# Laying x out by chunk, reordering the first loads and norms, and splitting the convolution's norm in a conditioned decoder block

## Chip, cores and metric

The kernel runs on all 8 cores of one Trainium2 chip. Each core computes one of the 8 sequences; the cores exchange nothing. The time is the device time of one launch in microseconds, that of the slowest core.

## The reference

For one sequence, x is 2048 x 1024 and c has 1024 entries. Weights are float32; the kernel multiplies in bf16.

```
mod = silu(c) @ w_ada + b_ada              # sh1 sc1 gt1 sh2 sc2 gt2, 1024 each
h   = rmsnorm(x) * (1 + sc1) + sh1         # norm1_g folded in
p   = h @ w_in                             # u_a u_b | g_b g_c v | gates A, B
u   = (u_a + b) * sigmoid(u_b + b)
y_a = silu(layernorm(causal_conv31(u))) @ conf_w_out + b
y_b = (g_b * causal_conv3(g_c * v)) @ sc_w_out
x   = x + gt1 * ((sigmoid(gA) * y_a + sigmoid(gB) * y_b) @ w_o)
h2  = rmsnorm(x) * (1 + sc2) + sh2
x   = x + gt2 * ((silu(h2 @ w_g) * (h2 @ w_u)) @ w_down)
out = rmsnorm(x)
```

## The kernel before

Everything is kept transposed: channels on the 128 partitions, positions along the free dimension. The 2048 positions are four chunks r = 0..3 of TU = 512, the 1024 channels eight tiles k = 0..7 (KD). One matmul multiplies a 128x128 weight tile with a 128x512 tile; eight of them, over k, make one PSUM bank. Six banks go round as a ring (`next_bank`); banks 6 and 7 belong to reductions and to junk outputs.

The order of work is written out by hand in `stages()`. `Sched` notes for every operation which buffers it reads and writes, and places semaphore waits on the engine that issues it; each engine then runs its own list strictly in order. DMAs are issued from SP (the hardware queue) and from POOL (the software queue, all weight loads, which read float32 and write bf16), so a wait in either list holds back the loads behind it. A buffer that overlaps another in the one arena waits for that one's readers.

The stages, with the names used below:

- **Startup.** `load_x(r, q)` brings half a chunk of x. `crit_load(k)` brings the 1 MB of w_ada for the shift and the scale of channel tile k; `crit_group(k)` multiplies it with silu(c) in two long VectorE products and makes `gm` and `mod` of tile k in two short ones. `in_sq(r)` squares a chunk, `in_red(r, b)` sums the squares with eight matmuls by ones and makes 1/rms (Ln, Exp) on ScalarE, `in_tmp` multiplies x by it, `in_h` applies scale and shift. While these h tiles appear, matmuls are streamed, four for each (k, r) of r = 0, 1 (line 585), with slot A as weights. Slot B (`load_half(1, q)`) is issued from POOL in iteration k = 5, and `u_unit(2, 0)` is the first group that needs it.
- **Units.** `u_unit(j, r)`: 16 matmuls and the sigmoid gate (`glu`). `sc_unit(j, r)`: 24 matmuls (g_c, v, g_b), the 3-tap convolution on VectorE (one TS, two STT) and two TTs. Chunks 2 and 3 are normed by `in_sq`, `in_red`, `in_apply` between units.
- **31-tap convolution.** `load_xsh(r)` copies u into shifted rows by 16 DMAs from SBUF to SBUF. `conv_a(r)`: four groups of 32 narrow matmuls (line 627), each evicted twice by ScalarE. `conv_b(r)`: the layer norm, 8 matmuls by ones, then a chain of VectorE and ScalarE to four Silu outputs, all emitted in one piece.
- **Gates.** 32 steps (m, r) of 24 matmuls. From the units `sc_unit(3, r)` on, `bg_step()` adds three small w_ada products to each step, with three ring buffers whose loads SP issues.
- **Reload.** x is read a second time into `xs` for the residual, eight 1 MB DMAs, one per channel tile, issued after `conv_b(3)`.
- **w_o.** `wo_units(r)`: eight groups; m < 4 uses slot A, the others slot B. Then the dense FFN and the final norm.

Of the kernel before, what the change touches and what calls it, by code (L numbers as in the profile page):

```python
# [164 lines left out]
def build_nc():  # L165
    nc = bass.Bass("TRN2", target_bir_lowering=False)
    din = lambda n, s: nc.dram_tensor(n, s, F32, kind="ExternalInput").ap()
    xT = din("xT", [1024, S])
# [9 lines left out]
    with ExitStack() as st:  # L178
# [30 lines left out]
        B_xs = [[sch.buf("xs%d_%d" % (k, r), O_XS + (k * S + r * TU) * 4, O_XS + (k * S + (r + 1) * TU) * 4)  # L209
# [44 lines left out]
        B_wada = [mbuf("wada%d" % i, O_WADA + i * 8192, 8192) for i in range(NWR)]  # L254
        wada_sem = [dsem("d_wada%d" % i) for i in range(NWR)]
        cact = f32ap(O_CBF, 1024); B_cact = xbuf("cact", O_CBF, 4096)
        junk = f32ap(M + O_JUNK, 1024); B_junk = mbuf("junk", O_JUNK, 4096)
# [134 lines left out]
        def load_xsh(r):  # L392
# [7 lines left out]
            sch.dma_group("sp", s_xsh, fns, reads=[B_u[j][r] for j in range(4)] +  # L400
# [13 lines left out]
        wada3_d = wada_d.rearrange("p (n k) -> p n k", k=1024)  # L414

        def crit_load(k):
            i = k % NWR
            dst = wada[i].rearrange("p (n k) -> p n k", n=2)
            sch.dma("sp", wada_sem[i], lambda e, i=i, k=k, dst=dst: e.dma_start(out=dst, in_=wada3_d[:, k:k + 9:8, :]),
                    writes=[B_wada[i]])  # L420

        def crit_group(k):
            i = k % NWR
            STT(junk, wada[i][:, 1024:2048], 1.0, cact, ALU.mult, ALU.mult, [B_wada[i], B_cact], [B_junk, B_sc[k]],
                accum_out=mod[:, 8 + k:9 + k])
            STT(junk, wada[i][:, 0:1024], 1.0, cact, ALU.mult, ALU.mult, [B_wada[i], B_cact], [B_junk, B_sh[k]],
# [127 lines left out]
        def stages():  # L554
# [11 lines left out]
            for k in range(4):  # L566
                crit_load(k)
# [526 lines left out]
```

How the kernel before makes its waits and increments, by code:

```python
    def _need(self, eng, tok):  # L60
        if tok is None:
            return
        key, val = tok
        if key == "pe" and eng == "pe":
            return
        if self.known[eng].get(key, 0) >= val:
            return
        self.known[eng][key] = val
        h = self.sems[key]
        self.ops[eng].append(lambda e, h=h, val=val: e.wait_ge(h, val))
# [27 lines left out]
    def op(self, eng, fn, reads=(), writes=()):  # L98
        self.deps(eng, reads, writes)
        self.cnt[eng] += 1
        tok = (eng, self.cnt[eng])
        h = self.sems[eng]
        self.ops[eng].append(lambda e, fn=fn, h=h: fn(e).then_inc(h, 1))
        self._mark(tok, reads, writes)
# [1 line left out]
    def pe_group(self, fns, reads=(), writes=()):  # L106
        self.deps("pe", reads, writes)
        self.cnt["pe"] += 1
        tok = ("pe", self.cnt["pe"])
        h = self.sems["pe"]
        for f in fns[:-1]:
            self.ops["pe"].append(lambda e, f=f: f(e))
        self.ops["pe"].append(lambda e, f=fns[-1], h=h: f(e).then_inc(h, 1))
        self._mark(tok, reads, writes)
# [1 line left out]
    def dma(self, eng, semkey, fn, reads=(), writes=()):  # L116
        self.deps(eng, reads, writes)
        self.dma_cnt[semkey] = self.dma_cnt.get(semkey, 0) + 16
        tok = (semkey, self.dma_cnt[semkey])
        h = self.sems[semkey]
        self.ops[eng].append(lambda e, fn=fn, h=h: fn(e).then_inc(h, 16))
        self._mark(tok, reads, writes)
        return tok
```

## Time and profile before

| | |
|---|---|
| three timed runs | 1004.63, 1006.46, 1032.09 us; median 1006.46 |
| the profiled execution's own time | 998.41 us |
| its span, slowest core (core 1) | 996.8 us; the cores 982.9 to 996.8 |
| PE busy | 895.1 us, 90% |
| VectorE (DVE), ScalarE (ACT) busy | 504.0, 278.1 us |
| the chain that ended last | PE 79%, DMA 8%, DVE 6%, ACT 2%, issue 2% |
| read from DRAM | 106.78 MB |

Rows of the timeline have the start, the duration of a run of like instructions, engine, line, output and input, count, and in brackets how long the engine had been idle before and what released it. A run may hold small gaps. Rows of a DMA issue have the size in the destination and the time from issue to landing. "Share" is that of 16 DMA engines.

### The profile page before, as it was taken

The page shows a single profiled execution, that of the slowest core. Times are in us where ns is not written, and L with a number is a line of the kernel's source. Part 1 is how long each engine was busy: PE and PEld are TensorE (multiplying, and loading weights), DVE is VectorE, ACT ScalarE, POOL GpSimd, SP SyncE. Part 2 cuts the span into 40 slices and gives each one's busy share as a digit, 9 for nine tenths or more (in the row PEclk, how much of TensorE's full clock was granted, in tenths as well). Part 3 has the DMA queues.
Part 4 walks back from the last instruction along what each step waited for, and adds up shares of the span by engine and source line. Part 5 has one row for each costly group of instructions (what it writes and reads, how often), then busy time and mean ns, then how long its engine had stood idle before and what let it go on. Part 6 is the DMA issues. An engine that isn't in the chain of part 4 may idle for free.

```text
span 996.8 us, 13447 instructions; the slowest of 8 cores (982.9 to 996.8 us)
## 1 busy us (share of the span) xinstructions
PE 895.1 (90%) x4416; PEld 399.3 (40%) x4416; DVE 504.0 (51%) x911; ACT 278.1 (28%) x415; POOL 23.7 (2%) x51
## 2 busy tenths in 40 slices
PE   0449696999899999998999999999999999999993
PEld 0114242444344444443443444444444444444441
DVE  1773645466686656663666223264113531135576
ACT  1443443445322232221554111100111001110242
POOL 0000010000000000000000000000000000000000
PEclk9999798999999999999999999999999999999997
DMA  8793339335654342535041332223122211110036
GB/s 226 249 258 99 86 75 181 87 87 210 198 137 98 89 100 79 122 93 124 1 85 33 75 74 65 53 50 67 32 43 41 44 33 33 32 32 1 1 106 232
DMA packets 43331, 92.99 MB, mean 93 GB/s; under 512 B 4352, under 2 KB 25088, under 8 KB 39424
## 3 DMA queue, kind: packets, MB, share of 16 engines
q1 hardware_dynamic: 38224, 60.57, 20.3%
q0 software_dynamic: 5040, 31.57, 17.9%
q8 instruction: 37, 0.61, 0.2%
q14 instruction: 30, 0.25, 0.1%
HBM read 106.78 MB, written 8.39 MB: 116 GB/s over the span
## 4 chain that ended last, share of the span: by engine, by line
PE 79%; DMA 8%; DVE 6%; ACT 2%; issue 2%; SPq 1%; DVEq 0%; ACTq 0%; POOL 0%; POOLq 0%
PE ps L347 74%; PE ps L627 3%; DVE arena L329 3%; DMA arena<-w 2%; DMA arena<-arena 2%; DMA arena<-xT 2%; PE ps L469 2%; ACT arena L326 2%; DVE arena L333 1%; DVE arena L336 1%; PE ps L441 1%; SPq L399 1%; DMA arena<-cb 1%; ACT L326 1%; DMA arena<-wada 1%
## 5 line engine op out<-in xcount | busy, mean ns | idle before, releaser
L347 PE MATMUL ps<-arena 128*128 128x512 bf16 x3744 | 820.0, 382 | 28.6 <-ACT arena L326 12.7
L347 PEld LDWEIGHTS ps<-arena 128*128 128x128 bf16 x3744 | 367.2, 98 | 479.8 <-issue 46.1
L329 DVE TENSOR_TENSOR arena<-ps,arena 128x512 bf16<-128x512 f32 (+1 forms) x156 | 107.4, 691 | 281.5 <-PE ps L347 221.3
L333 DVE SCALAR_TENSOR_TENSOR arena<-ps,arena 128x512 f32<-128x512 f32 (+1 forms) x208 | 155.7, 750 | 117.1 <-PE ps L347 98.4
L326 ACT ACTIVATE arena<-ps 128x512 f32<-128x512 f32 x108 | 63.5, 594 | 311.0 <-PE ps L347 309.2
L326 ACT ACTIVATE arena<-arena 128x512 bf16<-128x512 f32 (+2 forms) x160 | 103.8, 694 | 149.7 <-DVE arena L333 66.2
L326 ACT ACTIVATE arena<-ps,arena 128x512 f32<-128x512 f32 x124 | 82.6, 687 | 189.7 <-PE ps L347 114.4
L329 DVE TENSOR_TENSOR arena<-arena 128x512 f32<-128x512 f32 (+3 forms) x141 | 86.5, 639 | 43.0 <-ACT arena L326 24.7
L333 DVE SCALAR_TENSOR_TENSOR arena<-arena 128x512 f32<-128x512 f32 (+1 forms) x92 | 63.1, 699 | 10.7 <-ACT arena L326 7.3
L336 DVE SCALAR_TENSOR_TENSOR ps<-arena 128x256 f32<-128x256 f32 (+1 forms) x112 | 52.5, 468 | 13.2 <-DMA arena<-wada 6.1
L326 ACT ACT_TABLE_LOAD x23 | 29.5, 1283 | 60.1 <-PE ps L469 24.5
L627 PE MATMUL ps<-arena 128*32 128x512 bf16 x512 | 32.8, 418 | 14.1 <-DMA arena<-arena 9.6
L441 PE MATMUL ps<-arena 128*128 128x512 bf16 x32 | 10.9, 504 | 33.0 <-DVE arena L329 33.0
L627 PEld LDWEIGHTS ps<-arena 128*32 128x32 bf16 x512 | 15.7, 105 | 31.2 <-issue 21.6
L585 PE MATMUL ps<-arena 128*128 128x512 bf16 x64 | 17.7, 427 | 10.3 <-ACT arena L326 10.3
L352 POOL DMA_DIRECT2D arena<-w x22 | 11.7, 531 | 568.4 <-PE ps L347 561.4
L469 PE MATMUL ps<-arena 128*128 128x512 bf16 x64 | 16.8, 409 | 5.9 <-ACT arena L326 5.9
L340 DVE TENSOR_SCALAR arena<-arena 128x512 f32<-128x512 f32 (+2 forms) x33 | 15.8, 478 | 9.2 <-DMA arena<-vecs 5.5
L336 DVE SCALAR_TENSOR_TENSOR arena<-arena 128x1024 f32<-128x1024 f32 x16 | 19.6, 1222 | 0.8
L441 PEld LDWEIGHTS ps<-arena 128*128 128x128 bf16 x32 | 3.7, 119 | 39.1 <-issue 37.2
L336 DVE DVE_READ_ACCUMULATOR ps<-arena 128x1 f32 x112 | 15.8, 141 | 0.0
L585 PEld LDWEIGHTS ps<-arena 128*128 128x128 bf16 x64 | 6.2, 105 | 22.3 <-issue 17.9
(19 smaller groups left out, 34.6 us busy)
## 6 DMA issues: line engine op xcount, KB each, us to landing
arena<-w POOLq DMA_DIRECT2D x22, 1024.0 KB, 8.9
arena<-xT SPq DMA_DIRECT2D x16, 1024.0 KB, 12.0
arena<-wada SPq DMA_DIRECT2D x96, 128.0 KB, 2.4
arena<-arena SPq DMA_DIRECT2D x64, 130.0 KB, 2.8
arena<-wada SPq DMA_DIRECT2D x8, 1024.0 KB, 12.9
outT<-arena SPq DMA_DIRECT2D x32, 256.0 KB, 2.7
arena<-wd POOLq DMA_DIRECT2D x8, 768.0 KB, 6.8
arena<-wada SPq DMA_DIRECT2D x16, 256.0 KB, 3.6
```

The lines of the kernel that those rows point to most:

```text
L326: sch.op("act", lambda e: e.activation(out=out, in_=in_, func=func, **kw), reads=reads, writes=writes)
L329: sch.op(eng, lambda e: e.tensor_tensor(out=out, in0=in0, in1=in1, op=op), reads=reads, writes=writes)
L333: sch.op("dve", lambda e: e.scalar_tensor_tensor(out=out, in0=in0, scalar=scalar, in1=in1, op0=op0, op1=op1), reads=reads, writes=writes)
L336: sch.op("dve", lambda e: e.scalar_tensor_tensor(out=out, in0=in0, scalar=scalar, in1=in1, op0=op0, op1=op1, accum_out=accum_out), reads=r ...
L340: sch.op("dve", lambda e: e.tensor_scalar(out=out, in0=in0, scalar1=scalar1, scalar2=None, op0=op0), reads=reads, writes=writes)
L347: fns.append(lambda e, lt=lt, rh=rh, i=i: e.matmul(bank[b], lhsT=lt, rhs=rh, start=(i == 0), stop=(i == n - 1)))
L352: return sch.dma("pool", slot_sem[slot], lambda e: e.dma_start(out=dst, in_=src), writes=[slot_buf[slot]])
L399: fns.append(lambda e, dst=dst, src=src: e.dma_start(out=dst, in_=src))
L441: fns = [lambda e, k=k: e.matmul(bank[b], lhsT=ones_d, rhs=sq1[k], start=(k == 0), stop=(k == KD - 1)) for k in range(KD)]
L469: fns = [lambda e, k=k, t=t: e.matmul(bank[6], lhsT=ones_d, rhs=t.sq[k], start=(k == 0), stop=(k == KD - 1)) for k in range(KD)]
L585: sch.pe_group([lambda e, b=b, lt=lt, k=k, r=r: e.matmul(bank[b], lhsT=lt, rhs=hk(k, r), start=(k == 0), stop=(k == KD - 1))], reads=[B_h[ ...
L627: fns.append(lambda e, b=b, g=g, i=i, m=m: e.matmul(bank[b][32 * i:32 * i + 32, :], lhsT=stap[:, (g * 8 + m) * 32:(g * 8 + m + 1) * 32], r ...
```

## The change

- x lies in DRAM as `xc[r][partition][k, t]`, so half a chunk is 8 KB contiguous for a partition, and `xs` in SBUF has the same order (r, k, t).
- First loads: c, vecs, x(0), w_ada 0 and 1, x(1), w_ada 2 and 3 on SP, each w_ada load in two halves (scale first). Slot A's loads wait on POOL for the first half of x(1). Slot B's two loads are issued in iteration k = 6 after w_ada 6 landed. Then a chain of waits: x(2) after slot B's first half, slot E after x(2), x(3) after slot E.
- The w_ada products have two junk outputs, each half its own buffer; the two short operations go to POOL. `crit_group(0)` runs ahead of `in_tmp(0, .)`. The squares of chunk 1 are all on ScalarE. The streamed matmuls of chunk 1 lag those of chunk 0 (`lag`).
- `in_red(2)` and `in_apply(2)` are called inside `sc_unit(0, 0)`; `in_red(3)` and `in_apply(3)` only after the last `u_unit(j, 2)`.
- `conv_b(r)` puts six pieces into a list; `step()` runs one, twice in each `sc_unit` and once after each `u_unit(j, 3)`; `flush()` runs the rest. The order is now conv_a(r), then four `sc_unit`s. The first tap's product moves from VectorE to ScalarE.
- Slot A's second load waits on POOL for the shifted copy of chunk 1. SWO and CWO are loaded later.
- x is reloaded in four 2 MB DMAs, one after each of the gate steps m = 0..3, row r = m.
- w_o takes (m < 4, r = 0), (m < 4, r = 1), (m >= 4, r = 0), (m >= 4, r = 1).

```diff
+            crit_load(0)
+            crit_load(1)
+            tok_x1 = load_x(1, 0)
+            load_x(1, 1)
+            crit_load(2)
+            crit_load(3)
+            sch.wait_tok("pool", tok_x1)
+            load_half(0, 0)
+            load_half(0, 1)
             in_sq(0)
-            in_red(0, 6)
+            in_red(0, 7)
+            crit_group(0)
             for k in range(KD):
                 in_tmp(0, k)
-            in_sq(1)
+            in_sq(1, act_only=True)
             in_red(1, 7)
+            lag = {3: (0, 1), 4: (2, 3), 5: (4, 5), 6: (6,), 7: (7,)}
...
+                stream(k, 0)
+                for kk in lag.get(k, ()):
+                    in_h(1, kk, "dve" if kk == KD - 1 else "act")
+                    stream(kk, 1)
+                if k == KD - 2:
+                    sch.wait_tok("pool", tok_c6)
                     load_half(1, 0)
-                    load_half(1, 1)
+                    tok_w1 = load_half(1, 1)
+            sch.wait_tok("sp", (s_w8h[1][0], 16))
             load_x(2, 0)
-            load_x(2, 1)
+            tok_x2 = load_x(2, 1)
+            sch.wait_tok("pool", tok_x2)
+            tok_e = load_slot("E", w8_d[2])
+            sch.wait_tok("sp", tok_e)
             load_x(3, 0)
             load_x(3, 1)
-            load_slot("E", w8_d[2])
...
+            def hook2():
+                in_red(2, 6)
+                in_apply(2)
+            sc_unit(0, 0, hook2)
             sc_unit(0, 1)
             load_xsh(0)
             build_stap()
             u_unit(0, 2)
+            in_sq(3)
+            for j in range(1, 4):
+                u_unit(j, 2)
             in_red(3, 7)
             in_apply(3)
-            conv_a(0)
+            tok_xsh = conv_a(0)
+            conv_b(0)
             for j in range(4):
                 u_unit(j, 3)
+                step()
                 if j == 1:
+                    sch.wait_tok("pool", tok_xsh)
                     load_slot("A", w8_d[3])
...
+                if m < NR:
+                    sch.dma("sp", s_xr[m], lambda e, m=m: e.dma_start(out=xs[:, m * 4096:(m + 1) * 4096], in_=xc_d[m]),
+                            writes=[B_xs[k][m] for k in range(KD)])
...
+                if r == 0:
+                    order = [(m, 0) for m in range(4)] + [(m, 1) for m in range(4)] + [(m, 0) for m in range(4, KD)]
+                elif r == 1:
+                    order = [(m, 1) for m in range(4, KD)]
+                else:
+                    order = [(m, r) for m in range(KD)]
```

## Rows read from the trace of the kernel before

**Rows 1.** Spans and mean granted clock of two of the cores.

```profile
core 0: 984.0 us, clock 0.975
core 1: 996.8 us, clock 0.974
```

**Rows 2.** Stretches of core 1: length, busy PE, PEld, DVE, ACT, POOL, clock, DMA.

```profile
0.00:73.50 73.50, 24.88 (x80) 8.32 (x80) 39.02 (x78) 26.68 (x36) 3.94 (x15) 0.99 0.89 246
...
549.30:977.50 428.20, 428.17 (x1976) 193.70 (x1976) 167.58 (x248) 63.84 (x107) 7.92 (x15) 1.00 0.23 48
```

**Rows 3.** Timeline of core 1, PE alone, whole span.

```profile
22.63 3.57 PE L441 MATMUL ps<-arena 128*128 128x512 bf16 x8 [22.63 <-DVE arena L329]
...
73.53 21.82 PE L347 MATMUL ps<-arena 128*128 128x512 bf16 x88 [5.29 <-DMA arena<-w]
...
112.19 5.72 PE L347 MATMUL ps<-arena 128*128 128x512 bf16 x16 [9.93 <-ACT arena L326]
...
129.93 7.27 PE L627 MATMUL ps<-arena 128*32 128x512 bf16 x128
...
172.79 9.62 PE L627 MATMUL ps<-arena 128*32 128x512 bf16 x128 [9.59 <-DMA arena<-arena]
...
202.08 8.65 PE L627 MATMUL ps<-arena 128*32 128x512 bf16 x128 [2.30 <-ACT arena L326]
...
454.22 22.57 PE L347 MATMUL ps<-arena 128*128 128x512 bf16 x96 [4.67 <-DMA arena<-w]
...
549.33 402.43 PE L347 MATMUL ps<-arena 128*128 128x512 bf16 x1856 [3.48 <-DVE arena L340]
```

**Rows 4.** Timeline of core 1, startup.

```profile
29.14 7.31 DVE L329 TENSOR_TENSOR arena<-arena 128x512 f32<-128x512 f32 x12 [6.77 <-ACT arena L326]
...
42.39 1.22 DVE L336 SCALAR_TENSOR_TENSOR arena<-arena 128x1024 f32<-128x1024 f32 x1
...
43.72 1.23 DVE L336 SCALAR_TENSOR_TENSOR arena<-arena 128x1024 f32<-128x1024 f32 x1
...
59.76 1.06 POOL L369 DMA_DIRECT2D arena<-w  x2 [56.18 <-DVE arena L329]
```

**Rows 5.** DMA of windows 1.9:2.4, 20:30, 30:40, 248:249, 1:1.4 of core 1.

```profile
arena<-xT SPq DMA_DIRECT2D x1, 1024.0 KB, 16.4
...
q1 hardware_dynamic: 1315, 3.19, 100.4%
...
arena<-wada SPq DMA_DIRECT2D x1, 1024.0 KB, 6.8
...
arena<-w POOLq DMA_DIRECT2D x1, 1024.0 KB, 8.7
...
arena<-cb SPq DMA_DIRECT2D x1, 512.0 KB, 4.6
```

**Rows 6.** Timeline of core 0, PE alone, at its second convolution.

```profile
163.16 3.65 PE L627 MATMUL ps<-arena 128*32 128x512 bf16 x64 [1.39 <-ACT arena L326]
```

**Rows 7.** Timeline of core 1, norm of chunk 3 and evictions of the first convolution.

```profile
119.72 1.28 ACT L326 ACT_TABLE_LOAD   x1 [1.90 <-PE ps L441]
...
132.02 0.82 ACT L326 ACTIVATE arena<-arena 128x512 bf16<-128x512 f32 x1 [1.81 <-DVE arena L329]
132.74 5.87 ACT L326 ACTIVATE arena<-ps,arena 128x512 f32<-128x512 f32 x10
```

**Rows 8.** Timeline of core 1, conv_b(1), a gated-convolution unit, a background product.

```profile
189.93 0.68 DVE L333 SCALAR_TENSOR_TENSOR arena<-arena 128x512 f32<-128x512 f32 x1
...
200.64 0.81 ACT L326 ACTIVATE arena<-arena 128x512 bf16<-128x512 f32 x1 [0.59 <-DVE arena L329]
...
203.43 1.61 DVE L333 SCALAR_TENSOR_TENSOR arena<-arena 128x512 f32<-128x512 f32 x2
...
272.42 0.42 DVE L336 SCALAR_TENSOR_TENSOR ps<-arena 128x256 f32<-128x256 f32 x1
```

**Rows 9.** DMA of core 1 by issue, window 443.5:445.

```profile
arena<-wada SPq DMA_DIRECT2D x2, 256.0 KB, 14.9
```

More of the change, by code:

```diff
@@ new lines, in stream @@
+            def stream(k, r):
+                for blk in range(4):
+                    lt = slot_ap["A"][:, k * 512 + blk * 128: k * 512 + (blk + 1) * 128]
+                    b = r * 4 + blk
+                    sch.pe_group([lambda e, b=b, lt=lt: e.matmul(bank[b], lhsT=lt, rhs=hk(k, r), start=(k == 0), stop=(k == KD - 1))],
+                                 reads=[B_h[k][r], B_slh[0][k // 4]], writes=[B_bank[b]])
+            for k in range(KD):
+                if k > 0:
+                    crit_group(k)
+                if k + NWR < KD:
+                    tok = crit_load(k + NWR)
+                    if k + NWR == KD - 2:
+                        tok_c6 = tok
+                if k == 2:
+                    for kk in range(4):
+                        in_tmp(1, kk)
+                elif k == 3:
+                    for kk in range(4, KD):
+                        in_tmp(1, kk)
+                in_h(0, k, "act")
+                stream(k, 0)
[4 more added lines that the diff above has]
+                    sch.wait_tok("pool", tok_c6)
@@ L651, in conv_b @@
                         bias=vcol(C_LNB + j), scale=vcol(C_LNG + j))
+                pend.append(st_a)
+                pend.append(st_b)
+                for j in range(4):
+                    pend.append(lambda j=j: st_j(j))
             O_H1, O_H2 = 61568, 109824
@@ L747, in sc_unit, with in_apply @@
                 TT(vbuf[:, j * S + r * TU: j * S + (r + 1) * TU], bank[b], acc[i], ALU.mult, [B_bank[b], B_acc[i]], [B_v[j][r]])
[L749 to L750 removed]
+                step()
+            def in_apply(r, ks=range(KD)):
+                for k in ks:
                     in_tmp(r, k)
                     in_h(r, k, ("act", "pool", "dve", "act")[k % 4])
[L754 to L756 removed]
+            u_unit(2, 0)
+            u_unit(3, 0)
+            u_unit(2, 1)
             in_sq(2)
[L758 to L759 removed]
+            u_unit(3, 1)
+            def hook2():
+                in_red(2, 6)
+                in_apply(2)
+            sc_unit(0, 0, hook2)
             sc_unit(0, 1)
[L761 to L762 removed]
             load_xsh(0)
@@ L992, in stages @@
             down_stage(3, True)
-        s_xr = [dsem("d_xr%d" % k) for k in range(KD)]
+        s_xr = [dsem("d_xr%d" % r) for r in range(NR)]
         stages()
```

160 lines of the change are left out of this document (70 added, 90 removed).

## Prediction

> **What bounds the kernel now.** Spans first: core 1 ends 12.8 us after core 0 [rows 1], and the time is the slowest core's. Then the busy time by stretch: from 549.3 to 977.5 PE is busy without a gap, so nothing there can be gained by order, while of the first 73.5 us it is busy 24.9 [rows 2]. So I read PE's own timeline for its idle time and what ended it [rows 3]. A full-speed 512-column matmul takes 402.43/1856 = 0.217 us, and the 128 narrow ones of a convolution 7.3 us [rows 3]. The stages on core 1, with work counted in matmuls from the code:
>
> - Start to the first group that needs slot B: 73.5 us.
> - From there to the end of the four `u_unit(j, 3)`, at 137.2 + 64 x 0.217 = 151.0: 77.5 us for 256 matmuls (55.5) and one convolution (7.3), so 14.7 lost: 9.93 waiting for h of chunk 2, and slow matmuls behind the two waits (88 took 21.8 for 19.1, 16 took 5.7 for 3.5) [rows 3].
> - From there to the gates' first matmul, at 286.2 minus 44 matmuls and two 0.8 us bank waits, some 275: 124 us for 14 units, three convolutions and four reductions, 368 x 0.217 + 21.9 = 101.8, so some 22 lost. The largest is 9.59 for the shifted copy of chunk 1, with a cold convolution of 9.6 instead of 7.3 behind it; then 2.3 and slow again at conv_a(2) [rows 3]. Another 2 fall just after 275.
> - w_o: 4.67 waiting for slot B and 96 matmuls in 22.6 instead of 20.8, 6.4 together [rows 3].
>
> Core 0 waits for no copy at its second convolution, only 1.39 for ScalarE, and runs it at full speed [rows 6]: nearly all of its 12.8 us. So what the change removes there it removes from the cores that set the time.
>
> **Startup.** Three chains are near each other. Loads: the hardware queue alone moved 3.19 MB in 10 us, 3.3 us for 1.05 MB, and is in order [rows 5]. The first x half landed 16.4 us after its issue, since slot A's weights (two loads, 2 MB read) shared the engines and x rows came ahead of w_ada [rows 5]. Without them: c and vecs by about 6, x(0) 12, w_ada 0 at 15, w_ada 1 at 18, x(1) and half of slot A together to 27, w_ada 2 to 33, w_ada 3 to 36. VectorE: a long product starts every 1.33 us [rows 4]; with the junk outputs alternating and the short products gone I take 2.5 for a group against 3.35 minus 0.61 for `in_tmp` = 2.74 before. An `in_tmp` is 7.31/12 = 0.61 [rows 4]. Chunk 0: squares to 13, cold reduction 3.6 [rows 3], table load, Ln, Exp to 19.4, eight `in_tmp` to 24.5, group 1 to 27. Group 2 then waits for w_ada 2 at 33. From there six groups and eight `in_tmp`, 15 + 4.9 = 20, to 53.5. Group 6 ends at 51.
>
> That end is not what u_unit(2, 0) waits for. Slot B's two loads stand in POOL's list behind the short operations of group 6, so they leave at 51.5, not when w_ada 6 landed. Before they left at 59.76 and 60.3 [rows 4] and released PE at 73.5 [rows 3], 13 later; a load of the same bytes alone takes 8.7 [rows 5]. The second half meets the start of x(2), so I take 10: landed at 61.5, PE at 62. The stream itself would be done at 57 (short POOL operations, one `in_h`, eight matmuls, sigmoid). So PE is idle about 5 us again and pays the 2.7 of slow matmuls again. **Gain 11.5** (73.5 - 62), bounds 6.5 (the 13.0 again, and x(2) in the way) and 16 (the load hidden).
>
> The short POOL operations have no row here; the ends are 0.1 (a POOL memset) and 1.07 (a POOL operation on 512 columns), and I take 0.3, being one column: two for the last tile are on the path, 0.6, the others lie beside the next products. If they cost 1.07 each that is 1.5 more, inside the bounds.
>
> A page speaks against this move: the Trainium skill, SBUF — State Buffer, section SBUF: two separate sides, says that a VectorE operation with two SBUF inputs and a GpSimd one that reads SBUF exclude each other for a whole instruction. By that rule each short operation waits out a product of up to 1.2 us and each product a short operation; slot B's issue, behind group 6's pair, would come about 1 us later. No row of before has a one-column POOL operation beside a product.
>
> **To the end of u_unit(3, 3).** x(2) lands near 67, slot E (8.7, rows 5) near 76; sc_unit(0, 0) needs it at 62 + 2.7 + 13.9 = 78.6: in time by 2.6, and every microsecond beyond is PE's. Norm of chunk 2: reduction to 82, then ScalarE and VectorE as for chunk 3 before, table load at 119.7, last h at 132.8, of which 2.5 was VectorE doing other work [rows 7]: 10.5 net, to 92.5. PE has 7 groups to 90.6, so idle 1.9 in place of 9.93. Chunk 3 loses cover: its reduction now follows the last u_unit(j, 2), so only conv_a(0), 7.3, stands over the same 10.5: 3.2 idle. ScalarE evicts that convolution only behind `in_apply(3)`, 5.9 us for ten [rows 7], so the first piece of conv_b(0) waits some 1.5. With 1 for the squares of chunk 3 behind the 4.4 us table build and 2.7 + 1.5 of slow matmuls: 11.8 against 14.7, and 1.7 of reduction moved in. **Gain 3 to 4**, I take 4; bounds -2 (slot E late by 6) and 9. Three more table loads of 1.28 [rows 7] fall among the u_unit(j, 3); ScalarE has 11 us of work for 10.4 of PE's there, and the ring of banks takes that.
>
> **To the gates.** Slot A's load waits for the copy of chunk 1, SWO and CWO are queued behind slots A and B, and the next copies start after them, so the 9.6 and its slow convolution go. The whole of conv_b ran as a chain, 189.9 to 201.4 [rows 8], with PE short of banks behind it; in pieces, VectorE has per unit 2 x 0.7 + 1.6 + up to 2.6, 5.6 against PE's 5.2, and none in the fourth unit: 18.6 for 20.8. Late is only the last set, where three background products of 0.42 + 0.14 plus gaps, 1.8 a step [rows 8], meet the pieces: 25 for PE's 22.5, of which six banks hide about 2. I leave 1.5 of loss. **Gain 22** including the 2 behind 275; bounds 14 (each handover VectorE-ScalarE-VectorE of the first tap, about 0.5, shows in every unit) and 23.5.
>
> **Gates, reload.** The gates run without idle PE now, so they can only lose. A background load issued 5 us after a 2 MB reload stands behind 6 us of it, lands about 8.5 after the reload's issue, 3.5 after its own, and is wanted at 5.2: nothing lost. With a slot's load beside it (m = 1, 3) it is a few us late on VectorE, which has 3.9 of work in 5.2, and PE has its banks: I take 0, upper bound four times 3, since two background loads beside three slot loads took 14.9 [rows 9], 9.7 over the 5.2, of which the ring hides five banks of 1.3, some 6.5.
>
> **w_o.** Slot B's load leaves at the same point; four more groups with slot A, 6.9, now stand over the 4.67. The reduction of chunk 0 has four groups, 6.9, over its last square, which needs 1.8. **Gain 6.4**, bounds 5 and 6.5. The rest of the kernel is untouched.
>
> **Sum.** 11.5 + 4 + 22 + 6.4 = 44 to 45.5; with the 0.6 of POOL, 45. On the profiled execution's own 998.4 that is 953; its median stands 8 us higher, at 1006.5, and I see no part of those 8 that goes, so 961.
>
> **Rivals.** (1) The chain of startup waits is late: slot B's half, x(2), slot E follow each other, and each is stretched as before (13.0 for B, 16.4 for an x half). E lands 8 to 20 later and PE stands at sc_unit(0, 0): 961 + 8 to 20, centre 974. For it: 8 cores read at once and the rows above; against it: each load now has the queues to itself. (2) The reload does hold back the background products: 961 + 12 = 973. (3) Slot B hidden and slow matmuls gone: 961 - 5 - 3 - 3 = 950. (4) Small loads: w_ada comes in sixteen loads. A lone 512 KB load took 4.6 against 6.8 for a lone 1 MB [rows 5], so two in turn 9.2, 2.4 more, if not overlapped; 8 x 2.4 = 19, 980. The queue is full for all but the last two, which speaks against it. The Trainium skill, DMA: Bandwidth & Descriptors, section Anatomy of one DMA, puts about 2.0 us of fixed cost on every transfer. (5) Slower: the pieces do not spread but put their handovers on PE, because st_j's two TTs and a Silu stand in front of a unit's evictions. conv_b's 11.5 us four times and 0.9 for the first tap sixteen times are 60: 961 + 60 = 1021. It decides from 45 us, 3 us of every unit; six banks and an idle ScalarE (under half busy) speak against it. (6) The order changes but another wait ends at the same time everywhere: 1000.
>
> **Chances.** Forecast within 6 us: 0.42; (1) 0.19; (2) 0.12; (3) 0.18; (4) 0.03; (5) 0.03; (6) 0.03. About 2% is what a measurement of this kernel can tell from no change, so faster means under 986. Only the tail of (1), (5) and (6) miss that: faster 0.93, same 0.05, slower 0.02. The range takes in (3) at the bottom and most of (1) and (2) at the top: 947 to 979.
>
> **What would show it.** u_unit(2, 0) at 62, released by slot B's DMA; `in_red(0)` by 14; PE waiting about 2 before u_unit(0, 2) and 3 before u_unit(0, 3), on ScalarE; no wait on a DMA before a convolution or at w_o; gates starting near 238; cores within 3 us of each other instead of 13. Wrong would be: slot E as releaser at sc_unit(0, 0), background loads as releaser in the gates, or sc_units longer than 5.2.

## Result and the profile after

| | before | after |
|---|---|---|
| timed runs (median) | 998.82 to 1032.09 us (1005.55) | 966.93 to 969.43 us (968.98) |
| the profiled execution's own time | 998.41 us | 969.29 us |
| its span, slowest core | 996.8 us, core 1 | 967.7 us, core 4 |
| fastest core | 982.9 us | 957.7 us |

The ratio is 0.9654, 95% interval 0.9603 to 0.9705: 3.5% faster. The forecast was 961 with a range of 947 to 979. The 1032.09 is no part of the ratio: single executions in which one die ran at a lower clock are left out of every comparison and every median below.

The slowest and the fastest core of the kernel after, as [rows 1] for the kernel before:

```profile
core 4: 967.7 us, clock 0.970
...
core 6: 957.7 us, clock 0.982
```

PE alone, timeline of core 4 after, against [rows 3]:

```profile
16.50 3.35 PE L437 MATMUL ps<-arena 128*128 128x512 bf16 x8 [16.50 <-DVE arena L329]
...
63.93 15.61 PE L347 MATMUL ps<-arena 128*128 128x512 bf16 x63 [3.61 <-DMA arena<-w]
...
82.69 1.89 PE L347 MATMUL ps<-arena 128*128 128x512 bf16 x7 [3.14 <-DMA arena<-w]
...
97.15 15.66 PE L347 MATMUL ps<-arena 128*128 128x512 bf16 x63 [2.43 <-ACT arena L326]
...
125.56 27.41 PE L347 MATMUL ps<-arena 128*128 128x512 bf16 x117 [3.97 <-ACT arena L326]
153.51 3.64 PE L646 MATMUL ps<-arena 128*32 128x512 bf16 x64 [0.54 <-ACT arena L326]
157.64 3.65 PE L646 MATMUL ps<-arena 128*32 128x512 bf16 x64 [0.48 <-DVE arena L329]
...
183.77 7.11 PE L646 MATMUL ps<-arena 128*32 128x512 bf16 x128
...
213.37 7.12 PE L646 MATMUL ps<-arena 128*32 128x512 bf16 x128
220.64 32.14 PE L347 MATMUL ps<-arena 128*128 128x512 bf16 x145 [0.16 <-DVE arena L652]
255.84 1.01 PE L347 MATMUL ps<-arena 128*128 128x512 bf16 x2 [3.06 <-DVE arena L333]
...
332.56 114.94 PE L347 MATMUL ps<-arena 128*128 128x512 bf16 x514 [2.43 <-ACT arena L326]
...
520.05 402.43 PE L347 MATMUL ps<-arena 128*128 128x512 bf16 x1819 [3.48 <-DVE arena L340]
```

Read it from the back. The last row is that of before, 402.43 us, and begins 29.3 earlier: all of the gain lies ahead of it. The second convolution, at 153.51, waits 0.54 and 0.48 for ScalarE and VectorE and takes 3.64 + 3.65, where before stood 9.59 of waiting for a copy and 9.62 of slow convolution. The third and the fourth, at 183.77 and 213.37, wait for nothing and take 7.1; before, the third waited 2.30 and took 8.65. The 9.93 before the groups of chunk 2 is now 2.43, but 3.14 for slot E and 3.97 for chunk 3 are new, and so are 3.06 and 2.43 in the gates.

The prediction's stretches in the kernel after, as the windows of core 4 (length, busy PE, PEld, DVE, ACT, POOL, clock, DMA, GB/s), and then as a table beside those of core 1 before:

```profile
0.00:63.90 63.90, 26.11 (x79) 9.39 (x81) 34.98 (x59) 27.84 (x39) 17.11 (x29) 0.84 0.91 247
63.90:142.50 78.60, 68.82 (x387) 30.19 (x394) 40.34 (x57) 37.77 (x53) 5.04 (x7) 0.94 0.51 127
142.50:243.30 100.80, 98.93 (x737) 45.58 (x746) 65.66 (x107) 59.26 (x85) 2.37 (x7) 1.00 0.51 99
243.30:419.80 176.50, 169.73 (x753) 75.86 (x767) 109.82 (x290) 50.17 (x71) 2.36 (x5) 0.97 0.50 141
419.80:447.60 27.80, 27.64 (x128) 12.56 (x130) 12.72 (x18) 5.15 (x9) 1.35 (x3) 1.00 0.74 152
```

| stretch | before | after | gain | predicted |
|---|---|---|---|---|
| start to the first group with slot B | 73.5 | 63.9 | 9.6 | 11.5 |
| to the end of `u_unit(3, 3)` | 77.5 | 76.9 | 0.6 | 4 |
| to the gates | 124.0 | 102.5 | 21.5 | 22 |
| gates | 167.6 | 176.5 | -8.9 | 0 |
| 16 groups of w_o | 34.0 | 27.8 | 6.2 | 6.4 |
| sum | | | 29.0 | 43.9 |

The second stretch now holds eight matmuls of `conv_b(0)`, 1.7 us, which stood in the third before; the table books them there, so 78.6 - 1.7 = 76.9 and 100.8 + 1.7 = 102.5. The sum is the difference of the spans, 29.1. It is 15 short of the forecast, but the medians moved further: 36.6 as in the table, 35.7 without the 1032.09 (1004.63 to 968.98), since before's stands 6.2 above its profiled execution (998.41) and after's stands at its own.

**Where the gates lose.** 768 matmuls of 0.217 are 166.6; the stretch takes 9.9 more, before 1.0. VectorE, ScalarE and the issues of core 4 about the two waits show who is late (timeline, all engines):

```profile
243.58 0.53 POOL L352 DMA_DIRECT2D arena<-w  x1 [30.69 <-PE ps L347]
...
244.83 10.66 SPq L718 DMA_DIRECT2D arena<-wada  x6
...
253.40 0.43 DVE L336 SCALAR_TENSOR_TENSOR ps<-arena 128x256 f32<-128x256 f32 x1 [3.51 <-DMA arena<-wada]
...
319.42 0.33 SPq L875 DMA_DIRECT2D arena<-xc  x1
...
322.92 0.33 SPq L712 DMA_DIRECT2D arena<-cb  x1
...
328.50 1.28 ACT L326 ACT_TABLE_LOAD   x1 [6.10 <-DMA arena<-cb]
...
332.53 0.75 DVE L333 SCALAR_TENSOR_TENSOR arena<-ps,arena 128x512 f32<-128x512 f32 x1 [7.69 <-ACT arena L326]
```

At 243.58 POOL issues slot B's load, at 244.83 SP the small loads of the background products. VectorE reaches the product at 249.9, waits 3.51 in order for the load, and the banks it should free stop PE 3.06. At 319.42 SP issues a 2 MB reload, and 3.5 us later the second half of c; the Silu of it stands in ScalarE's list, waits 6.10, pays two table loads (the second at 330.44), and VectorE waits 7.69 behind it for the sigmoids: PE 2.43. In the view that sums the waits by what was waited for, VectorE's for small w_ada loads are

```profile
DVE ps L336 <- DMA arena<-wada: 20.1, 11, 4.9
```

20.1 us in 11 waits, of which the banks hide most.

**Startup.** Short operations on POOL, long products on VectorE, and slot B's issue (timeline of core 4):

```profile
44.98 1.22 DVE L336 SCALAR_TENSOR_TENSOR arena<-arena 128x1024 f32<-128x1024 f32 x1
...
45.23 3.30 POOL L423 TENSOR_SCALAR arena<-arena 128x1 f32<-128x1 f32 x1 [3.07 <-DVE arena L336]
...
47.27 1.22 DVE L336 SCALAR_TENSOR_TENSOR arena<-arena 128x1024 f32<-128x1024 f32 x1
...
48.50 0.19 POOL L329 TENSOR_TENSOR arena<-arena 128x1 f32<-128x1 f32 x1
...
48.78 6.00 ACT L326 ACTIVATE arena<-arena 128x512 bf16<-128x512 f32 x8 [4.30 <-POOL arena L329]
...
50.60 1.23 DVE L336 SCALAR_TENSOR_TENSOR arena<-arena 128x1024 f32<-128x1024 f32 x1 [0.73 <-DMA arena<-wada]
...
51.89 1.22 DVE L336 SCALAR_TENSOR_TENSOR arena<-arena 128x1024 f32<-128x1024 f32 x1
51.99 1.18 POOL L329 TENSOR_TENSOR arena<-arena 128x1 f32<-128x1 f32 x1 [1.44 <-DVE arena L336]
...
53.11 1.12 POOL L367 DMA_DIRECT2D arena<-w  x2
```

A one-column operation can take 0.19 on POOL (TENSOR_TENSOR) or 0.34 (TENSOR_SCALAR). The TENSOR_SCALAR at 45.23 takes 3.30, on all eight cores, while three products follow each other without a gap (44.98, one at 46.12, 47.27): it ends at 48.53, the last product at 48.49. The one at 51.99 takes 1.18 and ends with the product of 51.89. ScalarE waits 4.30 for the first. The Trainium skill, SBUF — State Buffer, section SBUF: two separate sides, says that, when the VectorE operation has two SBUF inputs and the GpSimd one reads SBUF, the later one waits for the whole instruction of the other; here it waits even through the instructions behind it. By that rule the prediction had slot B leave about 1 us later, and the trace agrees: 53.11, 1.0 after the pair of group 6 would end with 0.19 in place of 1.18.

The DMA view of the first 72 us of core 4 tells what the products themselves wait for: the loads of w_ada, 512 KB each, land 16.7 after their issue (the median), and the 16 engines are full to about 50 (a digit is 1.8 us):

```profile
DMA  0898999999999999999999999998208899999950
...
arena<-wada SPq DMA_DIRECT2D x16, 512.0 KB, 16.7
```

### The profile page after: what moved, and what is told of

Same layout as the page of the kernel before. It is cut to its first block, busy times and chain, and to the rows that moved or that the text cites. A ratio compares the mean times of both kernels' runs of the same rounds, so it can differ in the third digit from the quotient of the medians.

```text
span 967.7 us, 13419 instructions; the slowest of 8 cores (957.7 to 967.7 us)
## 1 busy us (share of the span) xinstructions
PE 889.5 (92%) x4335; PEld 399.4 (41%) x4416; DVE 490.9 (51%) x876; ACT 292.6 (30%) x437; POOL 37.2 (4%) x67
## 4 chain that ended last, share of the span: by engine, by line
PE 77%; DMA 11%; DVE 5%; ACT 3%; issue 3%; SPq 1%; DVEq 0%; POOL 0%; ACTq 0%; POOLq 0%
PE ps L347 74%; DMA arena<-wada 7%; DVE arena L329 2%; ACT arena L326 2%; DMA arena<-w 2%; PE ps L465 2%; DVE arena L333 1%; DMA arena<-xc 1%; PE ps L646 1%; ACT L326 1%; DVE ps L336 1%; DMA arena<-cb 1%; PE ps L437 0%; SPq L362 0%; SPq L412 0%
## 5 line engine op out<-in xcount | busy, mean ns | idle before, releaser
L347 PEld LDWEIGHTS ps<-arena 128*128 128x128 bf16 x3744 | 368.2, 99 | 474.9 <-issue 42.8
L326 ACT ACTIVATE arena<-arena 128x512 bf16<-128x512 f32 (+2 forms) x179 | 116.9, 694 | 159.6 <-DVE arena L329 72.6
L329 DVE TENSOR_TENSOR arena<-arena 128x512 f32<-128x512 f32 (+2 forms) x129 | 83.4, 667 | 33.6 <-ACT arena L326 19.9
L333 DVE SCALAR_TENSOR_TENSOR arena<-arena 128x512 f32<-128x512 f32 x84 | 61.3, 743 | 19.6 <-ACT arena L326 17.6
L336 DVE SCALAR_TENSOR_TENSOR ps<-arena 128x256 f32<-128x256 f32 (+1 forms) x112 | 52.4, 468 | 26.5 <-DMA arena<-wada 20.1
L437 PE MATMUL ps<-arena 128*128 128x512 bf16 x32 | 10.7, 496 | 26.2 <-DVE arena L329 16.5
L646 PE MATMUL ps<-arena 128*32 128x512 bf16 x512 | 28.6, 380 | 1.0 <-ACT arena L326 0.5
L437 PEld LDWEIGHTS ps<-arena 128*128 128x128 bf16 x32 | 3.6, 118 | 32.0 <-issue 30.1
L584 PEld LDWEIGHTS ps<-arena 128*128 128x128 bf16 x64 | 7.3, 117 | 20.3 <-issue 16.4
L465 PEld LDWEIGHTS ps<-arena 128*128 128x128 bf16 x64 | 6.5, 103 | 14.6 <-issue 8.0
## 6 DMA issues: line engine op xcount, KB each, us to landing
arena<-wada SPq DMA_DIRECT2D x16, 512.0 KB, 16.7
```

Source lines behind the costliest of these rows:

```text
L326: sch.op("act", lambda e: e.activation(out=out, in_=in_, func=func, **kw), reads=reads, writes=writes)
L329: sch.op(eng, lambda e: e.tensor_tensor(out=out, in0=in0, in1=in1, op=op), reads=reads, writes=writes)
L333: sch.op("dve", lambda e: e.scalar_tensor_tensor(out=out, in0=in0, scalar=scalar, in1=in1, op0=op0, op1=op1), reads=reads, writes=writes)
L336: sch.op("dve", lambda e: e.scalar_tensor_tensor(out=out, in0=in0, scalar=scalar, in1=in1, op0=op0, op1=op1, accum_out=accum_out), reads=r ...
L347: fns.append(lambda e, lt=lt, rh=rh, i=i: e.matmul(bank[b], lhsT=lt, rhs=rh, start=(i == 0), stop=(i == n - 1)))
L437: fns = [lambda e, k=k: e.matmul(bank[b], lhsT=ones_d, rhs=sq1[k], start=(k == 0), stop=(k == KD - 1)) for k in range(KD)]
```

## Experiments

Each kernel is named by its label; "before +" and "after +" say which kernel was edited. Ratios are to the kernel before on the same chip, with 95% intervals. The time is that of the slowest core, and which core that is changes from execution to execution. Where the time decides nothing, the mean of the eight cores' spans is given too, as its range over the executions. It varies less: 960.2 to 963.3 for the kernel after in four, and, beside the experiments, 988.9 to 994.5 for the kernel before in thirty-six.

**e1: is the gain to the gates the copy that waits?** Before +:

```diff
-            conv_a(0)
+            tok_xsh = conv_a(0)
...
                 if j == 1:
+                    sch.wait_tok("pool", tok_xsh)
                     load_slot("A", w8_d[3])
```

> The kernel before with one wait added: POOL issues slot A's second load, and behind it B, SWO and CWO, only after the shifted copy of chunk 1 landed. My account of the cores' 12.8 us: the copy's last transfers shared the DMA engines with four weight loads, so cores 1, 2, 4, 7 lose about 9.6 and 2.4 of slow matmuls. Then the wait of PE on the copy is gone on every core, the cores end within 4 us of each other, and the slowest ends 12 earlier: ratio 0.988. Rival: the weights are now late and the wait moves to sc_unit(1, 0), released by a weight load: ratio 0.995 to 1.00, and the cores still differ.

Measured 994.69, ratio 0.9908 (0.9881 to 0.9935). No core waits for a copy any more; the second convolution of core 4, a core that waited for its copy before, now has the row that [rows 6] had on core 0:

```profile
162.55 3.64 PE L627 MATMUL ps<-arena 128*32 128x512 bf16 x64 [1.39 <-ACT arena L326]
```

The mechanism is shown: one wait on POOL, ahead of weights that share the engines with the copy, takes PE's wait away and gives 0.9% of the kernel, 8 us and not the 12 of the account. The rest comes back further on, and the cores still differ by 9 (984.9 to 994.2), not by 4. Core 0, slowest here, waits 4.45 and 2.81 for ScalarE and VectorE just before the gates and 4.64 for slot B at w_o, where core 0 of the kernel before waits 1.93, 1.84 and 1.64. The first of these waits stands behind a load of half of c that SP issues behind the reload of x (ScalarE, core 0 here, then core 1 of the kernel before):

```profile
261.36 0.63 ACT L326 ACTIVATE arena<-arena 128x512 f32<-128x512 f32 x1 [13.81 <-DMA arena<-cb]
```

```profile
267.49 0.63 ACT L326 ACTIVATE arena<-arena 128x512 f32<-128x512 f32 x1 [10.27 <-DMA arena<-cb]
```

So the mean of the cores' spans falls by about 3 only, from 988.9 to 994.4 down to 987.2 to 989.6: the cores that waited for the copy gain, the others lose some. And the timed runs of this kernel lie within 2.6 (993.25 to 995.79), where 17 of the kernel before, run beside it, go from 998.25 to 1008.87: with the copy's wait goes most of the scatter of before's time.

**e2: w_o alone.** Before +:

```diff
-                for m in range(KD):
+                if r == 0:
+                    order = [(m, 0) for m in range(4)] + [(m, 1) for m in range(4)] + [(m, 0) for m in range(4, KD)]
...
+                for (m, r) in order:
```

> The kernel before with the new order of w_o alone. Account: no wait for slot B at w_o and no slow matmuls behind it, 6.4 on the slow cores and 1.7 to 2 on the others: ratio 0.994. Rival: the gap was also cover for something else (slots C and D, the background ring of the gt2 products), which is late next: ratio 0.998 to 1.00.

Measured 997.86, ratio 0.9951 (0.9911 to 0.9990), the runs from 992.91 to 1003.75: with the copy's wait still there they scatter as before's. The wait at w_o is gone on every core; on core 3 gates and w_o are one row:

```profile
294.11 184.05 PE L347 MATMUL ps<-arena 128*128 128x512 bf16 x852 [3.35 <-DVE arena L333]
```

**f4: the layout alone.** Before + x and its reload by chunk in DRAM, every order as before:

```diff
-            sch.dma("sp", s_x[r][q], lambda e: e.dma_start(out=dst, in_=xT3[:, q * 4:q * 4 + 4, R(r)]),
+            sch.dma("sp", s_x[r][q], lambda e: e.dma_start(out=xst[r][:, q * h:(q + 1) * h], in_=xc_d[r][:, q * h:(q + 1) * h]),
```

> The kernel before with x laid out by chunk in DRAM and nothing else moved: half a chunk is one run of 8 KB per partition instead of four of 2 KB. My prediction gave the layout nothing, since 2 KB rows already moved 3.2 MB in 10 us: then x(0) lands at 18 and 21 as before, and the ratio is 1.00. Rival: longer packets win x a larger share against the weight loads that run beside it, x(0) lands 2 to 4 earlier; but slot A's weights are then later and PE's first group waits for slot B anyway: still 0.998 to 1.00, with in_red(0) at 19 to 20 instead of 22.6.

Measured 1009.74, ratio 1.0072 (1.0042 to 1.0102): slower, which neither theory had. On core 2 the first two x loads land 15.4 after their issue instead of 17.3, but little of startup comes earlier: the first reduction is at 21.2 to 22.5 over the cores, before at 21.7 to 23.4, and not at 19 to 20 as the rival had it. The DMA view of the loads issued in 2 to 2.6 us of core 2 has

```profile
arena<-xc SPq DMA_DIRECT2D x2, 1024.0 KB, 15.4
arena<-w POOLq DMA_DIRECT2D x1, 512.0 KB, 15.0
```

and slot A's first half took 11.8 before. In the first 20 us the hardware queue moved 2.98 MB in 601 packets here, before 2.85 MB in 1388. It happens again to slot B (PE's timeline of core 2):

```profile
77.45 22.08 PE L347 MATMUL ps<-arena 128*128 128x512 bf16 x88 [9.92 <-DMA arena<-w]
```

Before, PE waited 5.29 for it and went on at 73.53 [rows 3]. Slot B's loads leave at 59.05 here and at 59.76 before, and land 15.0 and 11.4 after their issue. It is so on all eight cores: PE's wait is 9.4 to 10.3 where before it is 5.1 to 5.4, and the group starts at 76.3 to 78.3 instead of 72.1 to 73.7. These 4 us are half of what the ratio says. For the rest one cause is seen, not sized: six cores wait for the copy here (9.06 to 13.13), four in before's profiled execution. The Trainium skill, DMA: Bandwidth & Descriptors, section Queues, rings and completion order, lets every DMA engine alternate between queues packet by packet; longer packets on one queue then take time from the other. The rows agree with that, but nothing here was changed to test it alone. What is shown: with the old order the layout alone costs 0.7%, so none of the change's gain is the layout's by itself.

**e5: is the split norm worth its steps?** After +:

```diff
                 for j in range(4):
                     pend.append(lambda j=j: st_j(j))
+                flush()
```

> The changed kernel with every conv_b run whole at the point where it is called (all six pieces at once, behind conv_a), the order of units kept. My account: the pieces are what keeps PE fed; whole, each of the four norms puts its reduction and an 11.5 us chain of VectorE and ScalarE ahead of the next units' evictions, PE runs on through six banks and then stands some 3 to 5 us, four times: ratio 0.978, with PE released by ScalarE one to two units behind each conv_a. Rival: with four units between convolutions the chain has time enough anyway and the split is worth nothing: 0.966.

Measured 984.17, ratio 0.9837 (0.9795 to 0.9879), 15.2 above the kernel after. PE of the slowest core, behind the first convolution:

```profile
130.60 28.97 PE L347 MATMUL ps<-arena 128*128 128x512 bf16 x120 [8.19 <-DVE arena L652]
```

8.19 here against 3.97 in after, 4.2 more; behind each of the three later convolutions this timeline has waits of 1.47, 1.39 (the last time 1.90) and 0.56, where after has 0.2 or none: 3.4 to 3.9 each, 10.7. Together 14.9 of the 15.2. By the ratios, of the change's 3.46% e1's part is 0.92, w_o's 0.49 and the split's 1.83, 3.24 together, the first two good to about 0.3 and 0.4, the split's, a difference of two ratios, to about 0.7: next to nothing is left for startup and gates, and in the table above these are 9.6 + 0.6 - 8.9 = 1.3 us. Two companions of the split were not taken back alone: the four `sc_unit`s between two convolutions (three before) and the first tap's product on ScalarE.

**e3: the reload in pieces.** After + each 2 MB reload as four of 512 KB, one for each step:

```diff
-                if m < NR:
-                    sch.dma("sp", s_xr[m], lambda e, m=m: e.dma_start(out=xs[:, m * 4096:(m + 1) * 4096], in_=xc_d[m]),
...
+                    if m < NR:
+                        sch.dma("sp", s_xr[m * NR + r], lambda e, m=m, r=r: e.dma_start(
...
```

> The changed kernel with the reload of x in sixteen 512 KB pieces, one behind each gate step of m = 0..3, instead of four of 2 MB. If the 9 us that the gates lose on core 4 come from background loads that stand behind a 2 MB transfer, they shrink to about 3 (what stays is the first wait, beside slot B's load) and the ratio to before falls from 0.965 to 0.959. Rival: the loss comes from the slot loads beside the background loads, and from one wait for the second half of c; then the pieces change nothing: 0.965.

Measured 965.87, ratio 0.9626 (0.9574 to 0.9679). PE of the slowest core has one wait left from the gates to w_o, where after has two:

```profile
256.20 186.74 PE L347 MATMUL ps<-arena 128*128 128x512 bf16 x852 [3.80 <-DVE arena L333]
```

It is so on all eight cores; in after seven of the eight wait for ScalarE there (0.40 to 3.41). So the 2.43 behind the second half of c was the reload's. The median is 3.1 lower and the mean of the spans is 959.0 to 960.2; the intervals of the ratios overlap, so the verdict rests on the rows.

**f2: the other gate wait.** e3 + slot B's load behind the second gate step:

```diff
-            load_slot("B", w8_d[6])
...
+                    if m == 0 and r == 1:
+                        sch.wait_tok("pool", ("pe", sch.cnt["pe"]))
+                        load_slot("B", w8_d[6])
```

> The reload in sixteen pieces, and slot B's load for the gates (needed 41 us later) issued from POOL after the second gate step instead of before the first. The pieces alone took 3 of the 9 that the gates lose; in that run PE's one wait left in the gates, 3.8 and slow matmuls behind it, stood where the background loads share the engines with this slot load while VectorE is still behind with the norm's pieces. Account: two steps later VectorE has slack and six banks hide the same delay: 962 us, ratio 0.957. Rival: the wait moves with the load: 966.

Measured 965.75, ratio 0.9637 (0.9602 to 0.9672): nothing gained. The wait moved with the load:

```profile
268.01 175.02 PE L347 MATMUL ps<-arena 128*128 128x512 bf16 x804 [3.27 <-DVE arena L333]
```

From 256.20 to 268.01, as the rival said. It is not so wherever a 2 MB weight load and the small background loads meet. In e3 POOL issues three more slot loads in the gates, at 290.67, 332.11 and 373.55, and behind the first of them VectorE waits as long as at the start, but PE's row of 852 matmuls from 256.20 runs over all three (POOL and VectorE, core 7 of e3):

```profile
290.67 0.53 POOL L352 DMA_DIRECT2D arena<-w  x1 [46.94 <-PE ps L347]
...
301.87 0.43 DVE L336 SCALAR_TENSOR_TENSOR ps<-arena 128x256 f32<-128x256 f32 x1 [4.03 <-DMA arena<-wada]
```

There the banks take it. Why they don't in the first gate steps, and not two steps later either, stays open; nor was another arrangement (a deeper ring of small buffers, say) tried.

**e6: does slot E have to wait for x(2)?** After +:

```diff
-            sch.wait_tok("pool", tok_x2)
             tok_e = load_slot("E", w8_d[2])
```

> The changed kernel without POOL's wait for x(2) before slot E's load. On seven of the eight cores PE stands 0.8 to 3.3 at sc_unit(0, 0) for that load. Account: the serial chain (slot B's half, x(2), E) is longer than PE's 17 us of work beside it; without the wait E lands before 79 and the 3.1 goes: ratio 0.962. Rival: the three loads share the engines and all are late, slot B's second half by 3 among them, so PE starts at 67 and the chip is no faster: 0.965 to 0.968.

Measured 966.20, ratio 0.9662 (0.9625 to 0.9699). All 72 matmuls after slot B's wait run on, on every core (in after all eight waited, 0.86 to 3.31), and the reduction of chunk 2 starts at 79.25 instead of 84.41:

```profile
63.71 15.70 PE L347 MATMUL ps<-arena 128*128 128x512 bf16 x72 [2.08 <-DMA arena<-w]
```

The rival did not come: `u_unit(2, 0)` starts at 63.2 in the mean of the cores, in after at 63.1. The wait is gone, and the reduction of chunk 2 comes 3.2 earlier in that mean, as the account said. The median is 2.8 lower while the ratio is not, too little to tell by itself; but the mean of the spans, 957.0 to 958.9, lies below all of after's.

**e8: slot B earlier.** After + slot B's loads after w_ada 5 instead of 6.

```diff
-                if k == KD - 2:
-                    sch.wait_tok("pool", tok_c6)
+                if k == KD - 4:
+                    sch.wait_tok("pool", tok_c5)
```

> The changed kernel with slot B's two loads issued in iteration k = 4 after w_ada 5 landed, instead of k = 6 after w_ada 6. In its trace the DMA engines are full until 52, so startup is bound by bytes, not by VectorE as my prediction had it. If PE waits for B only because B is issued late, B lands about 4 earlier, the 3.6 wait goes and the ratio is 0.961. If bytes bound both, w_ada 6 and 7 come 3 later, the stream ends 3 later, and nothing is won: 0.964 to 0.966.

Measured 964.95, ratio 0.9673 (0.9599 to 0.9747). PE no longer waits for the slot, on any core:

```profile
62.13 13.97 PE L347 MATMUL ps<-arena 128*128 128x512 bf16 x64 [0.70 <-ACT arena L326]
```

It starts 1.8 earlier, not the 3.6 of its wait (1.2 in the mean of the cores): with the load hidden the stream of startup is itself the end. But slot B's landing also starts the chain of x(2) and slot E, and the reduction of chunk 2 comes 3.9 earlier in that mean. The mean of the spans is 957.2 to 959.2, below all of after's, though the ratio doesn't show it.

**e4: the short operations on VectorE.** After +:

```diff
-            sch.op("pool", lambda e: e.tensor_scalar(out=gm[:, k:k + 1]
+            sch.op("dve", lambda e: e.tensor_scalar(out=gm[:, k:k + 1]
```

> The changed kernel with the two short operations of each w_ada group on VectorE as before, instead of POOL. In the changed kernel's trace one of them takes 0.19 to 3.3 us on POOL, and ScalarE waits 5.6 and 4.3 for POOL. If these delays are what makes the stream end at 60.3 instead of 57, PE's first full group starts 1 to 3 earlier: ratio 0.963. Rival: VectorE's list is the chain, 0.38 a group come back on it, and slot B's load leaves 2 later: ratio 0.967.

Measured 967.92, ratio 0.9646 (0.9589 to 0.9702). On VectorE the pair takes 0.27 + 0.16, ScalarE waits for POOL no more, and slot B leaves at 51.66 instead of 53.11, now behind the landing of w_ada 6:

```profile
51.66 1.05 POOL L367 DMA_DIRECT2D arena<-w  x2 [25.08 <-DMA arena<-wada]
```

The streamed matmuls end at 58.7 instead of 60.3, and `u_unit(2, 0)` starts at 60.1 in the mean of the cores instead of 63.1, the reduction of chunk 2 2.6 earlier. So the account's 1 to 3 us came. In the median 1.1 is left of it, inside the noise; the mean of the spans is 959.2 to 960.8.

**e7 and f1: the reduction of chunk 3 earlier.** After + `in_red(3, 7)` between `u_unit(2, 2)` and `u_unit(3, 2)`; f1 + the table build moved behind `u_unit(2, 0)`:

```diff
             u_unit(2, 2)
+            in_red(3, 7)
             u_unit(3, 2)
-            in_red(3, 7)
             in_apply(3)
```

> The changed kernel with the reduction of chunk 3 ahead of the last u_unit(3, 2) and its apply behind it, so that 3.45 more of PE's work stands over the norm's chain. Account: the 4.0 that PE waits for h of chunk 3, and 1.4 of slow matmuls behind it, fall to about 1: ratio 0.961. Rival: the squares are not ready (VectorE is behind with the table build), the reduction itself waits, and PE stands before it instead: 0.965.

> The reduction of chunk 3 ahead of the last u_unit(3, 2), as in the run before, and the 4.4 us table build on VectorE moved from behind sc_unit(0, 1) to behind u_unit(2, 0), where VectorE is idle. In the run before, PE stood 3.9 at the reduction, since VectorE's squares were behind the table build, and another 3.2 later. Account: with the table out of the way the squares are ready, and of the changed kernel's 4.0 and 1.4 for chunk 3 about 1 is left: 965 us, ratio 0.963. Rival: the squares wait for x(3) itself, whose load is the last of the serial chain; then PE stands 3 to 4 at the reduction all the same: 969 to 972.

e7 measured 971.07, ratio 0.9719 (0.9671 to 0.9767), its median 2.1 above that of after. Its rival came: the squares of chunk 3 stand behind the table build on VectorE, and PE waits for them at the reduction instead, then twice more:

```profile
110.22 2.98 PE L437 MATMUL ps<-arena 128*128 128x512 bf16 x8 [3.92 <-DVE arena L329]
```

f1 measured 968.13, ratio 0.9662 (0.9627 to 0.9697). That wait is gone, and of the 3.97 in after 2.84 is left:

```profile
122.76 27.75 PE L347 MATMUL ps<-arena 128*128 128x512 bf16 x120 [2.84 <-ACT arena L326]
```

So the table build did hold back the squares; but the account's "about 1 is left" did not come, and what the 2.84 waits for is still ScalarE's norm. The gain of 0.9 is below what this many executions tell.

**f3: all that helped at once.** After + e3, e4, e6, e8, f1 and f2's later load.

> All together on the changed kernel: slot E without POOL's wait, slot B's first loads two groups earlier, the short operations on VectorE, the reduction of chunk 3 earlier with the table build moved, the reload in pieces and the gates' slot B load later. If the waits are separate their sizes add: 3 (slot E) + 3 (slot B and slow matmuls) + 4 (chunk 3) + 7 (gates) = 17: 952 us, ratio 0.948. If the startup ones are one wait for bytes, 5 of it do not come: 957.

Measured 958.69 (956.98 to 960.10), ratio 0.9567 (0.9538 to 0.9596): 10.3 below the kernel after and the fastest here. The intervals of f3 and of after don't overlap. PE of its slowest core, 957.4, and VectorE's last wait for w_ada there:

```profile
63.69 15.70 PE L347 MATMUL ps<-arena 128*128 128x512 bf16 x72
...
260.12 176.09 PE L347 MATMUL ps<-arena 128*128 128x512 bf16 x804 [4.50 <-DVE arena L333]
```

```profile
57.82 1.23 DVE L336 SCALAR_TENSOR_TENSOR arena<-arena 128x1024 f32<-128x1024 f32 x1 [2.93 <-DMA arena<-wada]
```

On this core u_unit(2, 0) still starts at 63.7, and one could read that nothing came earlier. The other seven start at 59.6 to 61.7 (after: 60.8 to 64.2 over all eight). The profiled executions of all runs give, as means over the eight cores:

| how much earlier than in after | `u_unit(2, 0)` | reduction of chunk 2 |
|---|---|---|
| e6, slot E | -0.2 | 3.2 |
| e8, slot B | 1.2 | 3.9 |
| e4, short operations | 2.9 | 2.6 |
| f3, all | 2.2 | 5.9 |

The kernels e3, f1 and f2, whose startup is that of after, reach the reduction 0.6 to 1.4 earlier, so these numbers are good to about 1. Neither of the two readings holds as it stands. Removed alone, each cause gave about its length, but the three together gave 5.9 and not 3.2 + 3.9 + 2.6 = 9.7: they overlap. Part of the overlap is bytes: with slot B's loads issued earlier VectorE waits 0.9 to 3.0 for the last load of w_ada, over the eight cores, where in after these waits are under 0.8. The 5.9 is still what the first reading gave startup (3 + 3). What it missed is behind: of chunk 3's wait 2.83 is left on this core, and the gates' first wait, 2.35 to 5.08 over the cores, is no smaller. That 957 came close, and 952 did not, is luck.

## Why the prediction was right

**To the gates, 22 predicted, 21.5 measured.** The copy's wait and its slow convolution went (e1), and the pieces keep PE busy (e5). The handovers on PE, rival (5), did not come: the units after the second convolution stand without a wait in PE's timeline.

**w_o, 6.4 predicted, 6.2 measured.** e2 shows it alone: the wait for slot B is covered by four more groups with slot A. There the median falls by 4.4, since the cores that don't wait for the copy have only 1.5 to 1.8 to lose at this place.

**Startup, 11.5 predicted, 9.6 measured.** Slot B was the releaser, as said, and PE waited 3.6 for it instead of 5. The way there was not as said. The prediction took VectorE's products for the bound from w_ada 2 on, ending at 53.5. They end at 54.4 on core 4, close to that, after five waits for loads of 4.5 in all; the 16 engines are full to about 50, so loads and products run out nearly together, and no run separates the two. What the prediction did not have is the tail behind them. The short POOL operation of 3.30 held ScalarE back by 4.30, the stream ended at 60.3 and not at 57, and slot B left at 53.1 and released PE 10.8 later, not 51.5 and 10; with the short operations on VectorE the stream ends at 58.7 (e4). `in_red(0)` came at 16.5, not 14: the second half of x(0) landed at 14.9, not 12. It had w_ada beside it, but that this was the cause is not shown. The term for the short POOL operations, 0.3 each, was mis-sized: 0.19 to 3.30.

**To the end of `u_unit(3, 3)`, 4 predicted, 0.6 measured.** The prediction's own terms add to 14.7 - 11.8 = 2.9, not 4. The step that failed is "in time by 2.6" for slot E. x(2) was issued only at 60.1, behind slot B's first half, so slot E left at 72.57 and landed 9.9 later, at 82.5 and not "near 76": PE waited 3.14 (gone in e6). That is rival (1) in small: its mechanism came, at its weak end, and cost 3, not 13. The two waits on ScalarE, predicted 1.9 and 3.2, were 2.43 and 3.97, both about 0.6 longer.

**Gates, 0 predicted, -8.9 measured.** The failed step is "with a slot's load beside it it is a few us late on VectorE ... PE has its banks: I take 0". The wait was 3.51 on VectorE, and the banks did not take it at the first slot load; at the three later ones they did, as the step says (e3). This is rival (2) for the most part: 8.9 of its 12. Its cause was half as stated: the reload is behind the second of the two waits, 2.43 (e3). The rest moved with slot B's load beside the small loads (f2), which is not the reload. What the prediction didn't see at all is c: one load in SP's list behind the reload, with ScalarE's whole list behind it. The trace of before had such a wait, for the first half of c, of 10.27 (under e1 above).

**The median.** On its own time the forecast was 953 and the execution took 969.3, 16 above it. The gains add to 11.5 + 4 + 22 + 6.4 = 43.9, and the 0.6 of POOL takes from that, so its own terms give 955; it took 45. The timed median came 8 above its forecast, not 16, because the 8 us by which before's median stood above its profiled execution were gone too. So half of the miss was made good by luck: the number is right within its range, and three of its five gains; the forecast of 961 within 6 us did not come, but a mixture of rivals (1) and (2), each at part of its price. The prediction saw "no part of those 8 that goes". They went with the copy's wait: e1 takes that wait away and its runs lie within 2.6, e2 leaves it and its runs spread over 11. The profiled execution of before was among its fastest, and the prediction took the step from it to the median for a constant.

Not as predicted either: the cores end within 10 us, not 3, and the gates start at 243.3, not 238. Left open: the order of the first loads was not run on the kernel before without the rest, and what makes one core slower than another in an execution is not known.

## What to carry to other kernels

Once PE is fed, look at what every small load is queued behind: a weight load of 2 MB or a reload beside them turns a list in order (VectorE for a product, ScalarE for one Silu) into a wait for all that follows, so cut the large load to the size of a step. For the reload this is shown (e3); for the weight load it was not tried. Where a copy or a last-minute load feeds PE, let the large loads with time to spare wait for it: one wait on POOL was worth 0.9% of the slowest core's time, though a third of that in the mean of the cores: what is held back comes later, and may make the next thing wait. When the time is that of the slowest of eight cores, judge a gain of 1 to 4 us by a milestone and a mean over all cores: from the slowest core alone e6, e8 and e4 looked like nothing, and each gave about 3 us. And don't add such gains: three that gave 9.7 one by one gave 5.9 together.

## What the hardware did that was not expected

- A layout with longer contiguous rows alone made the kernel 0.7% slower (f4): the weight loads on the software queue landed 3 to 4 us later (15.0 us for 11.8 from issue to landing for slot A's first half, 15.0 for 11.4 for slot B, core 2), and slot B released PE 3 to 5 us later on all eight cores.
- A one-column TENSOR_SCALAR on POOL took 0.34 us alone and 3.30, on all eight cores, beside three back-to-back products of 1.22 on VectorE, ending within 0.1 of the last of them. It and the TENSOR_TENSOR behind it, 0.19 alone, took 0.27 + 0.16 on VectorE (e4).
- The granted clock of PE fell to 0.54 of full, its lower level of 1.2 GHz, in 125.5 to 129 us of the kernel after, right behind the 3.97 us wait, and was 1.00 from 129 on: the row of 120 matmuls took 27.41 instead of 26.0, so 1.4 us were lost on top of the wait.
